# Attention of a two-layer decoder step: the mask goes into the score products, the exponentials read PSUM, GpSimd does the division, the first query block turns one key block

## The reference

```python
def sink_softmax(s, mask, sink):
    s = jnp.where(mask, s, -jnp.inf)
    m = jnp.maximum(jnp.max(s, axis=-1, keepdims=True), sink)
    p = jnp.exp(s - m)
    return p / (jnp.sum(p, axis=-1, keepdims=True) + jnp.exp(sink - m))

def swa_prompt(q, k, v, sinks):      # 16 heads of 64, 4 key heads, 4 query blocks of 128
    ...
    mask = (kpos >= 0) & (kpos <= qpos) & (qpos - kpos < WINDOW)
    s = jnp.einsum('bnqkgd,bnskd->bnkgqs', qb, kb).astype(jnp.float32) * scale
    p = sink_softmax(s, mask[None, :, None, None], sink)
    o = jnp.einsum('bnkgqs,bnskd->bnqkgd', p.astype(v.dtype), vb)
```

## Time and profile before

| what | value |
|---|---|
| median of three runs | 3251.42 us |
| profiled execution, its own time | 3249.49 us |
| its span, first to last instruction | 3247.7 us |
| PE busy | 3076.2 us, 95% |
| DVE busy | 2541.7 us, 78% |
| POOL busy | 1822.5 us, 56% |
| ACT busy | 1383.5 us, 43% |
| mean granted clock of PE | 0.967 |

### The profile page before, as it was taken

The page is one execution under the profiler, slowest core; times in us unless marked ns, Lnnn a source line. Parts: engine busy times, 40 slices in busy tenths (PEclk is TensorE's granted clock), DMA queues, the critical chain, the costliest instruction groups (busy, mean ns, idle before and its releaser), DMA issues.

```text
span 3247.7 us, 46734 instructions
## 1 busy us (share of the span) xinstructions
PE 3076.2 (95%) x17222; PEld 2785.8 (86%) x17222; DVE 2541.7 (78%) x4953; ACT 1383.5 (43%) x2559; POOL 1822.5 (56%) x1160
## 2 busy tenths in 40 slices
PE   7879999899999999999888899998999999999997
PEld 7879999899998887778775789998999988877776
DVE  7755999977765999999567358989777739989987
ACT  2522343467763333333244233343776643333332
POOL 4543488777773355655130223887777744556652
PEclk9999999899999999999888899999999999999998
DMA  3213499799998999999130122898999989999993
GB/s 109 72 52 96 149 334 337 277 395 391 397 378 318 401 400 399 401 397 379 53 97 1 33 66 79 309 341 298 362 384 398 398 311 396 398 402 399 399 401 136
DMA packets 286579, 920.92 MB, mean 284 GB/s; under 512 B 27344, under 2 KB 77392, under 8 KB 282688
## 3 DMA queue, kind: packets, MB, share of 16 engines
q1 hardware_dynamic: 154336, 415.63, 35.5%
q0 software_dynamic: 111280, 404.77, 32.9%
q10 hardware_dynamic: 20736, 97.53, 7.4%
HBM read 817.34 MB, written 102.38 MB: 283 GB/s over the span
## 4 chain that ended last, share of the span: by engine, by line
PE 68%; DVE 21%; DMA 6%; POOL 2%; issue 1%; ACT 1%; SPq 1%; DVEq 0%; ACTq 0%
PE ps L1682 29%; PE ps L1630 18%; PE ps L1556 10%; PE ps L1662 5%; DMA sring<-s_dram 4%; DVE rowsB L1122 2%; DVE rowsA L1122 1%; DVE cand L1211 1%; DVE cand L1218 1%; DVE slot L1224 1%; DVE xn L941 1%; DVE xl L934 1%; POOL low L597 1%; DMA rowsB<-u,pick 1%; PE ps L1804 1%
## 5 line engine op out<-in xcount | busy, mean ns | idle before, releaser
L755 ACT ACTIVATE high<-raw 128x1024 fp32r<-128x1024 f32 x512 | 542.5, 1059 | 963.6 <-PE ps L1682 638.0
L597 POOL TENSOR_TENSOR low<-raw,high 128x1024 fp32r<-128x1024 f32 x256 | 613.5, 2397 | 227.6 <-ACT high L755 221.3
L1630 PE MATMUL ps<-xh,high 128*128 128x384 f32 x2048 | 700.8, 342 | 10.1 <-POOL low L597 9.9
L1630 PE MATMUL ps<-xh,low 128*128 128x384 f32 x2048 | 688.2, 336 | 0.0
L1630 PE MATMUL ps<-xl,high 128*128 128x384 f32 x2048 | 687.1, 335 | 0.0
L1682 PE MATMUL ps<-high,hh 128*128 128x512 f32 x1536 | 486.6, 397 | 23.7 <-DVE low L1294 23.7
L1682 PE MATMUL ps<-low,hh 128*128 128x512 f32 x1536 | 482.5, 395 | 0.0
L1682 PE MATMUL ps<-high,hl 128*128 128x512 f32 x1536 | 481.1, 394 | 0.0
L588 POOL DMA_INDIRECT rowsB<-v,pick x192 | 289.6, 1508 | 274.5 <-DVE ps L1129 238.0
L588 POOL DMA_INDIRECT rowsA<-v,pick x192 | 300.3, 1564 | 221.2 <-DVE ps L1129 215.2
L1630 PEld LDWEIGHTS ps<-xh,high 128*128 128x128 f32 x2048 | 387.1, 189 | 14.3 <-POOL low L597 13.4
(11 more groups left out here) (279 smaller groups left out, 5146.7 us busy)
## 6 DMA issues: line engine op xcount, KB each, us to landing
raw<-uT SPq DMA_DIRECT2D x256, 512.0 KB
raw<-v SPq DMA_DIRECT2D x256, 512.0 KB
gate_dram<-gblk ACTq DMA_DIRECT2D x24, 2048.0 KB
gt<-gate_dram SPq DMA_DIRECT2D x32, 1536.0 KB
s_dram<-sring ACTq DMA_DIRECT2D x120, 384.0 KB
sring<-s_dram SPq DMA_DIRECT2D x120, 384.0 KB
raw<-wts SPq DMA_DIRECT2D x74, 512.0 KB, 3.6
rowsB<-u,pick POOLq DMA_INDIRECT x192
```

Source lines behind the costliest of these rows:

```text
L597: pool.tensor_tensor(low[:, m % 4], raw[:, m % 4], high[:, (m + 2) % 3].bitcast(F32), ALU.subtract).then_inc(sem("lo_ready"), 1)
L755: act.activation(high[:, (m + 2) % 3], tile_raw(m), ACT.Copy).then_inc(sem("hi_ready"), 1)
L1630: ins = pe.matmul(ps[:, m % 2, 0:DN], w[:, c], x[:, c, 0:DN], start=(c == 0 and k == 0), stop=(c == NC - 1 and k == 2))
```

## The change

It makes four edits. TensorE adds the mask: after each score product a second product, the identity (`identR`) times the mask (`maskR`), both F32R, is added into the same PSUM columns; DVE makes `identR`, `maskR` and the negated sinks `nsink` once, and PE waits for them. DVE takes the maximum straight from PSUM, unscaled, and no longer writes scores to `pr`; ACT's exponentials read PSUM, with the scale in the instruction, and write `pr`. So the bank pair is free only when ACT is done (`pexp`) and no longer when DVE is (`pmax`). The multiplication by the inverted sums moves from DVE to POOL (`weigh`). Units 0 to 3 work on 128 keys alone: half the transposes, half the copy of them, exponentials of 128 columns, no memset.

```diff
@@ POOL
+            def weigh(k):
+
+                p, m = pr[:, k % PRS], sm[:, k % PRS]
+                lo = 0 if k >= NKV else WIN
+                pool.wait_ge(sem("p_sum"), k + 1)
+                pool.tensor_tensor(p[:, :, lo:], p[:, :, lo:],
+                                   m[:, 5, 0:GRP].unsqueeze(2).broadcast_to([P, GRP, 2 * WIN - lo]), ALU.mult
+                                   ).then_inc(sem("p_ready"), 1)
             for l, (lo, hi) in enumerate(((0, W_K), (W_K, W_N))):
+                if l == 1:
+                    split_weights(W_K, W_O + 2)
+                    for k in range(UNITS):
+                        weigh(k)
+                    lo = W_O + 2
                 split_weights(lo, hi)
@@ ACT
                 def exps(u):
-                    act.wait_ge(sem("pmax"), item_of(u) + 1)
+                    lo = 0 if u >= NKV else WIN
+                    act.wait_ge(sem("pmax"), u + 1)
+                    if u >= PRS:
+                        act.wait_ge(sem("pturn"), u - PRS + 1)
                     for g in range(GRP):
-                        act.activation(p[:, g], p[:, g], ACT.Exp, bias=m[:, 1, g:g + 1],
-                                       accum_out=m[:, 2, g:g + 1])
+                        act.activation(p[:, g, lo:], sbank(item_of(u))[:, g // 2, (g % 2) * 256 + lo:(g % 2 + 1) * 256],
+                                       ACT.Exp, bias=m[:, 1, g:g + 1], scale=HD ** -0.5, accum_out=m[:, 2, g:g + 1])
...
+                    kb = 0 if u >= NKV else 1
+                    act.activation(prT[:, u % 2, GRP * kb:].rearrange("p (b j) k -> p b (j k)", b=2 - kb),
+                                   ps[:, 2 + kb:4, :], ACT.Copy).then_inc(sem("prT_ready"), 1)
@@ DVE
+                dve.tensor_copy(identR[:, :], ident).then_inc(sem("mask_ready"), 1)
+                dve.tensor_copy(maskR[:, :], atc[:, C_MP - C_COS:C_MS - C_COS]).then_inc(sem("mask_ready"), 1)
+                dve.tensor_scalar(nsink[:, :], prm[:, P_SINK:P_SINK + NH], -1.0, None, ALU.mult
+                                  ).then_inc(sem("mask_ready"), 1)
+                dve.wait_ge(sem("mask_ready"), 3)
...
                     if u >= PRS:
-                        dve.wait_ge(sem("pturn"), u - PRS + 1)
-                    chain.did(dve.scalar_tensor_tensor(
-                        p[:, :, lo:], sbank(k).rearrange("p b (g k) -> p (b g) k", g=2)[:, :, lo:],
-                        HD ** -0.5, atc[:, C_MP - C_COS + lo:C_MP - C_COS + 2 * WIN].unsqueeze(1).broadcast_to([P, GRP, w]),
-                        ALU.mult, ALU.add))
-                    if not n:
-                        chain.did(dve.memset(p[:, :, 0:WIN], BIG))
-                    chain.settle()
-                    chain.did(dve.tensor_reduce(m[:, 0, 0:GRP], p, X, ALU.max))
-                    chain.settle()
-                    sk = prm[:, P_SINK + kv * GRP:P_SINK + (kv + 1) * GRP]
-                    chain.did(dve.tensor_tensor(m[:, 0, 0:GRP], m[:, 0, 0:GRP], sk, ALU.max))
-                    chain.settle()
-                    chain.did(dve.tensor_scalar(m[:, 1, 0:GRP], m[:, 0, 0:GRP], -1.0, None, ALU.mult))
-                    chain.settle()
-                    dve.tensor_tensor(m[:, 3, 0:GRP], sk, m[:, 0, 0:GRP], ALU.subtract
+                        dve.wait_ge(sem("p_ready"), u - PRS + 1)
+                    chain.did(dve.tensor_reduce(
+                        m[:, 0, 0:GRP], sbank(k).rearrange("p b (g k) -> p (b g) k", g=2)[:, :, lo:], X, ALU.max))
+                    chain.settle()
+                    heads = slice(kv * GRP, (kv + 1) * GRP)
+                    chain.did(dve.scalar_tensor_tensor(m[:, 1, 0:GRP], m[:, 0, 0:GRP], -HD ** -0.5, nsink[:, heads],
+                                                       ALU.mult, ALU.min))
+                    chain.settle()
+                    dve.tensor_tensor(m[:, 3, 0:GRP], m[:, 1, 0:GRP], nsink[:, heads], ALU.subtract
                                       ).then_inc(sem("pmax"), 1)
 
-                def normalise(u):
-                    p, m = pr[:, u % PRS], sm[:, u % PRS]
+                def inverse(u):
+
+                    m = sm[:, u % PRS]
                     dve.wait_ge(sem("pexp"), u + 1)
                     chain.did(dve.tensor_tensor(m[:, 4, 0:GRP], m[:, 2, 0:GRP], m[:, 3, 0:GRP], ALU.add))
                     chain.settle()
-                    chain.did(dve.reciprocal(m[:, 5, 0:GRP], m[:, 4, 0:GRP]))
-                    chain.settle()
-                    dve.tensor_tensor(p, p, m[:, 5, 0:GRP].unsqueeze(2).broadcast_to([P, GRP, 2 * WIN]),
-                                      ALU.mult).then_inc(sem("p_ready"), 1)
+                    dve.reciprocal(m[:, 5, 0:GRP], m[:, 4, 0:GRP]).then_inc(sem("p_sum"), 1)
@@ PE
                     for g in range(GRP):
-                        ins = pe.matmul(sbank(k)[:, g // 2, (g % 2) * 256 + lo:(g % 2 + 1) * 256],
-                                        qR[:, kv * GRP + g, n * WIN:(n + 1) * WIN],
-                                        kR[:, kv, ks:(n + 1) * WIN], start=True, stop=True)
+                        o = sbank(k)[:, g // 2, (g % 2) * 256 + lo:(g % 2 + 1) * 256]
+                        pe.matmul(o, qR[:, kv * GRP + g, n * WIN:(n + 1) * WIN], kR[:, kv, ks:(n + 1) * WIN],
+                                  start=True, stop=False)
+                        ins = pe.matmul(o, identR[:, :], maskR[:, lo:], start=False, stop=True)
...
                 def item(k):
-                    if k >= 2:
-                        pe.wait_ge(sem("pmax"), k - 1)
+                    if S_ITEM <= k - 2 < S_ITEM + 2:
+                        pe.wait_ge(sem("s_scaled"), k - 2 - S_ITEM + 1)
+                    elif k >= 2:
+                        pe.wait_ge(sem("pexp"), k - 2 + 1 - 2 * (k - 2 > S_ITEM))
...
-                    for kb in range(2):
+                    for kb in range(0 if u >= NKV else 1, 2):
...
+                pe.wait_ge(sem("mask_ready"), 3)
                 for k in items_due(-1):
```

More of the change, by code:

```diff
@@ L314, in decoder @@
         smS = st.take("smS", [P, 6, NB])
+        identR = st.take("identR", [P, P], F32R)
+        maskR = st.take("maskR", [P, 2 * WIN], F32R)
+        nsink = st.take("nsink", [P, NH])
         st = Span(nc, free_at, SB_HI)
@@ L882, in attention @@
                         act.wait_ge(sem("p_out"), u - 1)
-                    act.activation(prT[:, u % 2].rearrange("p (b j) k -> p b (j k)", b=2), ps[:, 2:4, :],
-                                   ACT.Copy).then_inc(sem("prT_ready"), 1)
+                    kb = 0 if u >= NKV else 1
+                    act.activation(prT[:, u % 2, GRP * kb:].rearrange("p (b j) k -> p b (j k)", b=2 - kb),
+                                   ps[:, 2 + kb:4, :], ACT.Copy).then_inc(sem("prT_ready"), 1)
                     if u + 2 < UNITS:
@@ L1394, in scale_max @@
                     lo = 0 if n else WIN
-                    w = 2 * WIN - lo
                     dve.wait_ge(sem("p_scores"), k + 1)
                     if u >= PRS:
-                        dve.wait_ge(sem("pturn"), u - PRS + 1)
-                    chain.did(dve.scalar_tensor_tensor(
-                        p[:, :, lo:], sbank(k).rearrange("p b (g k) -> p (b g) k", g=2)[:, :, lo:],
-                        HD ** -0.5, atc[:, C_MP - C_COS + lo:C_MP - C_COS + 2 * WIN].unsqueeze(1).broadcast_to([P, GRP, w]),
-                        ALU.mult, ALU.add))
-                    if not n:
-                        chain.did(dve.memset(p[:, :, 0:WIN], BIG))
+                        dve.wait_ge(sem("p_ready"), u - PRS + 1)
+                    chain.did(dve.tensor_reduce(
+                        m[:, 0, 0:GRP], sbank(k).rearrange("p b (g k) -> p (b g) k", g=2)[:, :, lo:], X, ALU.max))
                     chain.settle()
-                    chain.did(dve.tensor_reduce(m[:, 0, 0:GRP], p, X, ALU.max))
+                    heads = slice(kv * GRP, (kv + 1) * GRP)
+                    chain.did(dve.scalar_tensor_tensor(m[:, 1, 0:GRP], m[:, 0, 0:GRP], -HD ** -0.5, nsink[:, heads],
+                                                       ALU.mult, ALU.min))
                     chain.settle()
-                    sk = prm[:, P_SINK + kv * GRP:P_SINK + (kv + 1) * GRP]
-                    chain.did(dve.tensor_tensor(m[:, 0, 0:GRP], m[:, 0, 0:GRP], sk, ALU.max))
-                    chain.settle()
-                    chain.did(dve.tensor_scalar(m[:, 1, 0:GRP], m[:, 0, 0:GRP], -1.0, None, ALU.mult))
-                    chain.settle()
-                    dve.tensor_tensor(m[:, 3, 0:GRP], sk, m[:, 0, 0:GRP], ALU.subtract
+                    dve.tensor_tensor(m[:, 3, 0:GRP], m[:, 1, 0:GRP], nsink[:, heads], ALU.subtract
                                       ).then_inc(sem("pmax"), 1)
-                def normalise(u):
-                    p, m = pr[:, u % PRS], sm[:, u % PRS]
+                def inverse(u):
+                    m = sm[:, u % PRS]
                     dve.wait_ge(sem("pexp"), u + 1)
@@ L1445, in sample_scale @@
```

(4 more changed lines are left out.)

## The result

The changed kernel takes 3282.63 us (median of 6 runs, 3275.11 to 3288.42), the kernel before 3252.46 (6 runs beside them): a ratio of 1.0095, 95% interval 1.0080 to 1.0109. That is slower by 30 us, where 3256.5 was forecast and 3264 was the range's upper end. The profiled execution took 3280.71, its span 3278.9, which is 31.2 above the span before.

What follows compares the result with a forecast made beforehand. Attention units: first wait for DVE at low clock, 6 to 8 wait a little, 9 to 12 PE-bound. Terms 1.3 - 4.0 + 1.0 + 2.7 + 2.0 + 0.5 + 2.5 = +6.0; forecast 3256.5, range 3246 to 3264.

Steps and rivals of the forecast that it cites:

- the price of the mask products: Four mask products per attention unit on PE: 0.49 us a unit at full clock, 0.9 at half, 0.55 for units 0 to 3.
- Front, +1.3: Start of the attention piece: copy of qS and three small DVE steps now precede PE's first scores, +1.3 us.
- To the scores of unit 4, -4.0: First scores to unit 4's: waits go (-4.2), two transpose groups halved (-2.0), four mask groups added (+2.2); together -4.0 us.
- Units 6 to 8: Transposes there wait 0.5, 0.5 and 1.5 us behind the 4.0 chain over POOL; with three masks, +2.7.
- Units 14 and 15: Transposes have only sample products beside the chain: 2.2 us of wait each instead of 0.94, together +2.5.
- Units 9 to 12: PE's own work, 4.26 us, exceeds the chain's 4.0; PE-bound at 7.0 a unit instead of 6.50, together +2.0.
- PE never waited for the exponentials: Scores two units ahead now wait for ACT's `pexp`; wait forecast at nothing, 1 us a unit were ACT late by 1.
- The clock: First units: transposes raise PE's clock by the trace, so halving them may delay the rise a unit; not in the sum.
- the mask products cost as much as score products: Rival: mask products 1.5 us dearer in some nine units that hide nothing, +13, giving 3269; chance 0.03.
- The clock is lost: Rival: new waits or weaker first units bring four more half-clock stretches on PE, +6.5 us, giving 3263; chance 0.18.
- Won early: Rival: PE reaches 2.4 GHz by unit 3's scores, giving back about 6 us: 3250.5, no change; chance 0.09.
- DVE was the bound: Rival: DVE's step shrinks by half, so 14.0 us of PE idle before the transposes go: -8.7, 3242; chance 0.10.

Runs made afterwards that it cites:

- mask first: Changed kernel with the mask written first, one 128-row product per two heads, the four score products adding to it: 3260.3, ratio 1.0010.
- all rows alike: Changed kernel with `kR` and `qR` widened by 64 partitions of zeros, so score products have 128 rows like the mask products: 3243.1, ratio 0.9974.

## Why the prediction was wrong

The step that failed is the price of the mask products: "Two such products of 288 columns start 0.26 after the two before, 0.13 each; 256 columns make 0.12, so 0.49 a unit at full clock, 0.9 at half". The row is right, and a mask product behind another one did add 0.12. But all products of the earlier trace rows have 128 rows (128*128 in the rows), while the score products of the earlier trace rows have 64 (64*128); in the new order the array goes from one to the other eight times a unit instead of twice, at about 0.2 a change. A unit's mask took 1.76 at full clock, 2.4 (128 keys) and 2.8 (256 keys) at half. It lay inside the ends that the prediction itself had set, nothing and 1.99; the point taken, 0.49, was the price without the changes. Where the rows did not change, that price came: 0.48 a unit with 64 rows (2.40 - 1.92) and 0.48 with 128 (2.31 - 1.83). Over the piece the masks cost 26.9 (161.2 - 134.3), where 7.1 were booked. The whole mask with two changes a unit left 8.1 of it, near the 7.1 (mask first, 142.4 - 134.3); half of the mask left 1.1 (135.4 - 134.3, one run), and the whole mask in two halves, with a product more a head, 16.4 (150.7 - 134.3). So 18.8 belong to the six changes more and to the time at 1.2 GHz that goes with them, by the kernel with the same columns in all.

The Trainium skill, page "TensorEngine Tiling (Array Packing)", section Tiling Modes (Key Properties), states that changing the tiling mode drains TensorE, as going to another tile does not. It gives no price. No run here shows that a product of 64 rows counts as another mode than one of 128; if it does, the traces agree: a load that waits 0.33, 0.1 to 0.2 a change, and nothing where rows stay alike. The prediction had read the two shapes in its rows and not asked what lies between them.

By its other steps:

- Front, +1.3: the first scores start 1.25 after the copy of qS does (1688.75 to 1690.00), and not 0.03 after it. Right.
- To the scores of unit 4, -4.0: it became +3.5 (1690.00 to 1716.09, against 22.63). Four mask groups at 2.4 and not 0.55 are 7.5 more. The rest of the step was right: the waits there went and the transposes were halved.
- Units 6 to 8, waits of 0.5, 0.5 and 1.5 behind the chain over POOL: none in the changed kernel, since PE itself was later. With the mask off PE they stood there, 0.39, 0.45 and 1.41. The mechanism was right, the sizes by luck: for unit 8 the forecast set 2.48 of scores with mask beside a chain of 4.0, and what gave 1.41 were 1.99 of scores alone beside a chain of 3.40 (1748.86 to 1752.26). POOL took 1.89, not 2.4; and the 2.78 of the earlier trace rows was not "beside a busy DVE", which worked 0.53 us in it, and 0.93 in the 2.34. (Of the waits before, the row puts the 0.59 down to ACT's copy of `pssN`, not to this chain.)
- Units 14 and 15, 2.2 each: 1.65 and 1.65, by POOL's shorter step.
- Units 9 to 12 bound by PE, 7.0 each: bound by PE, but 8.2 (1768.00 to 1776.19). With all rows alike it is 6.83 (1759.05 to 1765.88).
- PE never waited for the exponentials in the changed kernel: right. (Without the masks the scores of unit 2 did, 1.20.)
- The clock, "by the trace transposes raise it", and with four of them the rise may come a unit later: not shown. In the stretch named PE also multiplied with V. The rise did come later in the changed kernel, 44.9 us after the first scores and not 30.2 as before, but not by the halved transposes: with them and without masks on PE it came after 13.1 (mask and division on DVE) and 13.8 (mask left out).

Of the rivals, "the mask products cost as much as score products" was nearest, with 0.03, and its sign came (groups of 3.68). Its price, 1.5 more a unit, was near the 1.3 by which a unit at full clock came out dearer (1.76 against 0.49); it left out the half clock, where the difference is 1.9. "The clock is lost" was half right: PE was at 0.50 between units 6 and 11 (1779.5 to 1782.5), but with no wait before it. "Won early" failed in the changed kernel (0.50 up to 1734.5). It came true where the score products had 128 rows, and for a while in the kernels without masks on PE (mask left out, mask on DVE, mask and division on DVE): there 2.4 GHz came before the scores of unit 4, was lost again after some 10 us, and the piece kept 0.75 to 0.77. "DVE was the bound" fell with the division. How the 18.8 divides between the changes and the clock is not settled: a longer unit also stands longer at 1.2 GHz.

## What to carry to other kernels

Before a product is put between others on TensorE, compare the rows of both operands in the profile (the 64*128 beside the 128*128): a stream that alternates paid 0.1 to 0.2 us at each change here (0.2 beside F32R masks, 0.13 beside float32 masks, 0.11 in the sample products), as much as a pass of 256 columns (0.12) or more. Pad the short operand with zeros, group products of like rows, or split the tall one; the padding costs no columns. And price an operation from a row whose neighbours are those that it will have.

## What the runs showed that was not expected

- Score products of 128 rows, half of them zeros, stood with an earlier 2.4 GHz than the same ones of 64 rows: after 3.5 us (mask on PE) and 4.9 us (mask on DVE) instead of 16.0 and 12.7 (1687.10 to 1699.8), and PE's first rows have the same durations in the narrow and the wide kernel. Each is one profiled run. It came in all three wide kernels (3.5, 3.5 and 4.9), and their pieces had 0.90 to 0.92 where the others had 0.72 to 0.82. All runs together fit it: the mean granted clock of the whole span, over 10, 6 and 6 runs, was 0.973 in each of the three, and 0.963 to 0.969 in the other kernels with six runs or more. Why more rows go with an earlier rise is open.
- PE fell to 1.2 GHz without a pause before it: 27.0 us of unbroken work at 1.00 up to 1779, then 3 us at 0.50.
- The kernel before had the same cost in its own sample products, 8 rows beside 128, 0.11 each on 64 products, in rows that the prediction had used as fixed work.
